# A hybrid decoder step on one core: where a chunk's own products stand among the query products of the chunked scan

## The reference, cut to what matters

```python
m = (C @ B^T) * exp(segsum(da)) * dt          # inside the chunk
y_diag = m @ x                                # from the chunk's own tokens
y_off  = exp(da_cs) * (C @ state)             # from the state left by the chunks before
state  = exp(da_cs[-1]) * state + B^T @ (w_end * x)
y = (y_diag + y_off + d_skip * x) * silu(z), then an RMS norm
```

## Time and profile before

| what | value |
|---|---|
| median of three runs | 1590.19 us (1589.43 to 1591.71) |
| profiled execution: its time, its span | 1590.01 us, 1588.2 us |
| the scan's loop | from about 292 to 379 us of the span |
| PE busy, weight loads busy | 88 %, 71 % of the span |
| DVE, ACT, POOL busy | 57 %, 42 %, 10 % |

### The profile page before, as it was taken

One profiled execution on the slowest core, in us unless ns is written; L12 is line 12 of the kernel. 1 busy time (PEld: TensorE's weight loads), 2 busy tenths in 40 slices (PEclk: granted clock), 3 DMA queues, 4 the chain that ended last, 5 costly groups with the idle time before them and its releaser, 6 DMA issues. The chain is left out here.

```text
span 1588.2 us, 23221 instructions
## 1 busy us (share of the span) xinstructions
PE 1393.3 (88%) x8147; PEld 1126.9 (71%) x8147; DVE 912.4 (57%) x1368; ACT 664.5 (42%) x951; POOL 151.5 (10%) x245
## 2 busy tenths in 40 slices
PE   3999999798489888997777998399999999977997
PEld 2888999687276667665445887278888888863786
DVE  3331654677266664333224455598889989843564
ACT  3333224331133332222114221288877887744442
POOL 1110000232000000000000100010000000000451
PEclk9999999898699997999988999599999999998999
DMA  7315120222424442265526553559876799945451
GB/s 218 114 57 157 40 54 30 106 101 80 139 68 102 112 116 83 67 177 166 168 60 217 196 192 146 198 203 389 329 256 218 249 390 399 396 155 214 149 169 54
DMA packets 147140, 267.41 MB, mean 168 GB/s; under 512 B 24161, under 2 KB 75746, under 8 KB 146706
## 3 DMA queue, kind: packets, MB, share of 16 engines
q1 hardware_dynamic: 138098, 233.46, 44.0%
q0 software_dynamic: 5760, 20.97, 3.8%
q10 hardware_dynamic: 3168, 11.54, 1.8%
HBM read 215.06 MB, written 50.87 MB: 167 GB/s over the span
## 5 line engine op out<-in xcount | busy, mean ns | idle before, releaser
L2353 DVE TENSOR_TENSOR low_gate<-raw_gate,high_gate 128x2048 fp32r<-128x2048 f32 x44 | 99.3, 2289 | 34.3 <-ACT high_gate L2270 34.2
L2353 DVE TENSOR_TENSOR low_down<-raw_down,high_down 128x2048 fp32r<-128x2048 f32 x44 | 98.8, 2288 | 15.6 <-ACT high_down L2270 15.6
L2353 DVE TENSOR_TENSOR low_up<-raw_up,high_up 128x2048 fp32r<-128x2048 f32 x44 | 98.9, 2287 | 4.0 <-ACT high_up L2270 2.1
L1220 PE MATMUL pb<-kh,qh 128*128 128x512 f32 (+2 forms) x192 | 77.3, 516 | 19.1 <-DMA vh<-v_d 19.1
L1372 PE MATMUL pb<-cst,pages 128*128 128x128 f32 x512 | 73.4, 308 | 23.3 <-DMA pages<-in_cache 19.9
L2270 ACT CAST high_gate<-raw_gate 128x2048 fp32r<-128x2048 f32 x44 | 82.2, 1909 | 16.8 <-DMA raw_gate<-in_w_gate 16.8
L1372 PEld LDWEIGHTS pb<-cst,pages 128*128 128x128 f32 x512 | 66.8, 160 | 31.5 <-DMA pages<-in_cache 23.8
L1266 ACT ACTIVATE prob<-pb,nmx 128x128 f32<-128x128 f32 (+3 forms) x64 | 47.4, 741 | 92.8 <-DVE nmx L1294 92.8
L469 PE MATMUL pb<-hH,blkH 128*128 128x344 f32 x264 | 84.5, 320 | 0.0
L470 PE MATMUL pb<-hL,blkH 128*128 128x344 f32 x264 | 84.3, 319 | 0.0
L471 PE MATMUL pb<-hH,blkL 128*128 128x344 f32 x264 | 84.3, 319 | 0.0
(11 more groups left out here) (427 smaller groups left out, 3439.0 us busy)
## 6 DMA issues: line engine op xcount, KB each, us to landing
pages<-in_cache SPq DMA_DIRECT2D x256, 144.0 KB, 2.4
raw_gate<-in_w_gate SPq DMA_DIRECT2D x32, 1024.0 KB, 9.8
raw_up<-in_w_up SPq DMA_DIRECT2D x32, 1024.0 KB, 10.6
raw_down<-in_w_down SPq DMA_DIRECT2D x32, 1024.0 KB, 8.8
y_d<-yo ACTq DMA_DIRECT2D x22, 512.0 KB
raw<-in_w_in SPq DMA_DIRECT2D x17, 512.0 KB, 4.0
y_d<-zero SPq DMA_DIRECT2D x16, 512.0 KB, 4.3
xt<-in_x_all SPq DMA_DIRECT2D x9, 512.0 KB, 4.8
```

The source lines that it names most:

```text
L1220: last = pe.matmul(pb[:, 2 * (t % 2) + a // 512, 0:w], qh[n][:, i * P:(i + 1) * P], kh[n][:, a:a + w], start=True, stop=True)
L2353: dve.tensor_tensor(part(low_[w], c), part(raw[w], c), part(high[w], c).bitcast(F32), ALU.subtract).then_inc(S(w + "_low"), 1)
```

## The change

In each turn PE runs `back(j)` ahead of all three query thirds, where it stood behind the first. On DVE `chunk_back(j)` moves ahead of the first third and of `weights(j+1)`, and the three thirds follow together. No instruction, operand, wait or DMA is added or removed.

```diff
@@ PE, L554
             for j in range(PT):
                 if j + 1 < PT:
                     front(j + 1)
-                queries(j, 0)
                 back(j)
-                queries(j, 1)
-                queries(j, 2)
+                for ch in range(NC):
+                    queries(j, ch)
@@ DVE, L1074
                     masked(j + 1)
                     if j + 2 < PT:
                         steps(j + 2)
-                queries(j, 0)
+                chunk_back(j)
                 if j + 1 < PT:
                     weights(j + 1)
-                chunk_back(j)
-                queries(j, 1)
-                queries(j, 2)
+                for ch in range(3):
+                    queries(j, ch)
```

## The result

The change makes the kernel slower: 1600.11 us as the median of five runs (1595.73 to 1602.79) against 1589.43, also of five, for the kernel before, ratio 1.0072 with an interval of 1.0051 to 1.0092. The forecast was 1591.9 in a range that ended at 1594.9. Medians and ratios leave out runs in a slower state, of which there was one, 2079.33 us among e7's four.

What follows compares the result with a forecast made beforehand. DVE's chain from dec to dec was taken as the bound, PE's own work nearly equal. -2.35 + 3.75 + 0.33 = +1.7 on the profiled 1590.01 gave 1591.7, with the median 0.18 above it 1591.9 us; range 1588.6 to 1594.9.

Steps and rivals of the forecast that it cites:

- What bounds the kernel now: Loop: the chain through DVE from dec to dec ends last; PE's own work is 10.65 of 10.80 us.
- A steady turn: Each turn, dec to dec: the chain grows by 0.75 us to 11.55, +3.75 over five turns.
- xdt 0.60: Term in the steady turn's sum: DVE's xdt step takes 0.60 us, start to start.
- The sentence that cost POOL's products at nothing: Loop: POOL's xw and skip term cost nothing, each having several us of cover in a turn.
- The first turn: First turn: back(0) fills PE's 3.75 us idle gap; next dec at 304.50 instead of 306.84, -2.35.
- The branch that the forecast chose for the clock: First turn: PE, working on without the gap, is at its upper clock for back(0); -2.35 us taken, not -1.55.
- The last turn: Last turn: back(7) waits for mT; the last third ends 1.73 us later, 0.33 of it this turn's.
- The rival of the falling clock: Loop: PE's 0.9 us idle per turn drops the clock; one turn +9, all six some +54; chance 0.04.
- The row against it: Profile window 270 to 284, cited against a falling clock: PE busy 10.32 of 14 us, clock kept 1.00.

Runs made afterwards that it cites:

- e7: Changed kernel with 26 matmuls, results thrown away, on PE in the wait ahead of chunk 2's dec; 1599.05 us as median of three, ratio 1.0067.
- e5: Changed kernel with DVE's weights (xdt, mT of the next chunk) put ahead of chunk_back; 1586.68 us, ratio 0.9995.
- e9: e5 with POOL's xw also waiting for st1; 1585.99 us, ratio 0.9978.
- e8: Changed kernel with POOL's skip product held back until its chunk's mT is made and xw until st1; 1592.75 us, ratio 1.0021.
- e1: Changed kernel with POOL's skip product of the next chunk held back until that chunk's mT is made; 1593.54 us, ratio 1.0039.
- e2: Kernel before with one extra POOL product per turn, on tiles no DVE loop instruction uses, started to run beside xdt; 1590.69 us, ratio 1.0019.
- e3: Kernel before with only PE's order changed (back ahead of all three query thirds), DVE's order kept; 1622.87 us, one run.

## Why the prediction was wrong, step by step

**What bounds the kernel now**: right. The chain through DVE sets the turn, PE's own work lies 0.2 below it: with the chain shortened (e5, e9) the turn is 10.59.

**A steady turn**: the chain was right (L1050 waits 0.82 for L524, as forecast), one term was mis-sized. "xdt 0.60" was taken from a row beside which POOL ran only the root's two steps on one column (0.19 and 0.94, from 321.35 on); behind L1062 it is 1.45, start to start (330.62 to 332.07). 11.55 + 0.85 = 12.40, which is what turns 2, 4 and 5 take within 0.01; turn 3 takes 12.74. The sentence that cost POOL's products at nothing went wrong: it asked whether they would be late, not whom they would run beside. The trace of before had shown it, ahead of the loop, in the first row of the timeline of DVE from which the prediction was made; it was passed over. There xdt ran between POOL's xw and its skip product, and mT behind it took 2.06 in place of 1.22:

```profile
284.07 1.20 DVE L1038 TENSOR_TENSOR xdt<-xrow,dt 128x512 f32<-128x512 f32 x1
...
285.20 2.06 DVE L1042 TENSOR_TENSOR mT<-mT,gm 128x1024 f32<-128x1024 f32 x1
...
283.11 1.62 POOL L631 TENSOR_TENSOR xw<-xrow,wend 128x512 f32<-128x512 f32 x1 [3.80 <-ACT xrow L797]
284.69 1.48 POOL L636 TENSOR_TENSOR xskip<-xrow,brow 128x512 f32<-128x512 f32 x1
```

The Trainium skill, SBUF — State Buffer, section Who interferes with whom, states the rule: a DVE instruction with two inputs in SBUF contends with a GpSimd (here POOL) instruction that reads SBUF, the ports that they share are an exclusive lock, and the order of issue decides who blocks; with at most one input in SBUF a DVE instruction does not contend, outside of certain modes. The traces agree: xdt and st1 take 1.53 beside POOL, while the state's sum and L1055, which read PSUM, take 0.69 and 0.68 beside xw at 327.93.

**The first turn**: 2.35 were forecast, 0.81 came (17.59 against 18.40). PE did fill its gap with `back(0)`, but st1 beside xw and xdt beside the skip product took 1.53 each in place of 0.68, and the two cost 1.6 together: e8, without them, has 15.96, the forecast's 16.06 to 0.1. The branch that the forecast chose for the clock came true: from 297.00 to 303.40 the changed kernel ran at 1.00, and `back(0)` ended at 298.07, before DVE came to st1 at 298.64.

**The last turn**: right but for xdt in the turn ahead of it, 0.85. From the last dec to the loop's end it is 21.41 before, 22.59 in the changed kernel and 21.77 in e1 and e8: +0.36 without the clash, where 0.33 were forecast.

**The rival of the falling clock** had a chance of 0.04 and happened, in one turn: 14.82 against 12.40 makes 2.4, not the 9 that I reckoned for a whole turn, as the clock was back within some 5 us. The row against it (a window with PE busy three quarters, at 1.00) averages over short gaps and says nothing of one gap of 4 us, and the forecast did not price that gap in turn 1 at all; its sum has 0.9 of idle PE for each turn, and e8, which runs as that sum has it, waits 2.50 there. The Trainium skill, TensorE: Matmul & The Clock Gate, section A second HAM failure mode: psum-queue depth-cycling, warns that short idles between groups of matmuls, where they are frequent, make the clock swing. It was borne out in part: in the changed kernel the clock fell behind the wait of 4.09 and held through those of 1.57 to 1.92.

The sum of what was missed: 1.53 up to the second dec (both clashes of turn 0), 3.27 in turn 1 (0.85 and the clock's 2.4), 3.72 in turns 2 to 5 (four times 0.85, and 0.35), 0.85 in turn 6: 9.4, and 1.7 + 9.4 = 11.1, as measured in the profiled execution. Of the 9.4 some 6.6 are the clashes and 2.4 the clock.

**Open**: what lets the clock fall behind one wait and not behind a longer one; the 0.35 ahead of L1058 in turn 3 of the changed kernel, and alike in e1 and e8, where the trace names only DVE's own step before; and why the runs of e1 and e5 come out slower than their traces: e1's loop ends 2.7 later than before while its ratio makes 6.2, and e5's ends 3.2 earlier while its ratio makes 0.8. The clock in their other executions is not known.

## What to carry to other kernels

When a step moves on DVE, look not only at what it waits for but at what POOL does at its new place: the duration of an instruction with both inputs in SBUF, read in a row without a wide POOL step beside it, holds only where none will run beside it. Put such steps where the engine would wait anyway, and POOL's work beside steps that read PSUM. And where two loops are within a few per cent of each other, price the idle that a longer chain gives PE: it can cost clock as well as time.

## What had not been expected of the hardware

DVE's 512-column product with both inputs in SBUF took 1.20 us (e2) in place of 0.68 beside a POOL product on other tiles and 1.53 in the changed kernel, and POOL's own product 1.55 in place of 1.04 where it began behind such a step of DVE; DVE's ended 0.55 after POOL's in both e2 and the changed kernel, which looks like a turn taken, not a path shared. The granted clock fell behind waits of 1.94 to 4.58 us and held behind one of 3.60; behind waits of 3.26 to 3.28 in e3 it did both.
